# Moving the high and low planes of x into one buffer with longer rows, beside a smaller descriptor scratch

## The chip, the cores and the metric

The kernel runs on one core of a Trainium2 chip. The metric is the device time of one execution in microseconds. Three executions of the kernel before took 2121.49, 2124.33 and 2121.76 us; the median is 2121.76 us.

## What is computed

One step of a decoder layer over 264 tokens: 256 of a prompt and 8 of a sample group. Cut to what matters:

```python
proj = einsum('bld,dk->blk', h, w_in)          # 2048 features -> pool, z, xBC, dt, two gates
pooled = multiscale_pool(u); branch_a = (pooled @ w_pool * pool_scale) @ w_pool_br
y = ssd_chunked(conv(xbc), dt, a, ...) * silu(z), RMS-normed; branch_b = y @ w_ssd_br
out = (sigmoid(g_pool) * branch_a + sigmoid(g_ssd) * branch_b) @ w_out
x = layer_norm(ALPHA * x + out)                # then cross-attention into 256 memory tokens
x = layer_norm(ALPHA * x + attention(x))
x = layer_norm(ALPHA * x + (silu(x @ w_gate) * (x @ w_up)) @ w_down)
```

All of it is float32. The time goes into the products with the large weight matrices; the scans, convolutions and norms run beside them.

## The kernel before, in words

**Layout.** Activations lie feature-major: a feature is a partition, and the 264 tokens lie along the partition. The 2048 features of x are 16 tiles (KT), so x is `[128, 16, ...]`. In what follows a *row* of such a buffer is one tile's stretch of tokens within a partition.

**Products in three parts.** To keep float32 accuracy with the single-pass fp32r format, each operand is split into a high part and the rest, and a product is three matmuls (`mm3`, L392 to L396): x's high row with the weights' high part (L394), x's low row with the same high part (L395), x's high row with the weights' low part (L396). In each the 128x128 block of weights is the stationary operand (an LDWEIGHTS ahead of the matmul) and the row of 264 tokens is the moving one.

**Weights.** 688 units of weights of 128x1024 values (4096 bytes in a partition) stream through a ring of four slots: SyncE loads `raw`, ScalarE rounds it to `whi` (L863), VectorE subtracts to `wlo` (L1390). A unit (L398) is 8 blocks of 128 columns, so 24 matmuls; it waits for `lo_ready` once at its start. In most units 4 rows of x meet two output tiles each (`block_units`, L412), so a row is used by 6 matmuls one after another: high, low, high for one output tile, and again for the other. In the B and C projections a unit takes 8 rows for one output tile (L427).

**The buffers that move.** `xH` and `xL` (L217, L218) are the high and low parts of x: each `[128, 16, 268]` values, rows of 1072 bytes. The last four values of a row are two spare ones and the two gain and bias columns, which 768 of the matmuls take as two more moving columns (266 instead of 264). They are written by ScalarE (`xH`: L872, L1121, L1126, L1133) and VectorE (`xL`: L1405, L1862, L1869, L1923), and read again by VectorE in the residual (L1801, L1803) and the shift (L1824, L1826). Other moving operands of the same three-matmul scheme are `yH`/`yL`, `mixH`/`mixL`, `hH`/`hL`, `oH`/`oL` (rows of 1056 bytes) and `memH`/`memL` (256 tokens, rows of 1024 bytes).

**Addresses in a partition.** The program reserves 8192 bytes at address 0 for the descriptors of DMAs that GpSimd issues (`dynamic_dma_scratch_size`), 128 bytes of constants follow, and then the buffers in the order of `alloc` (L214 on): `raw`, `whi`, `wlo` of 16384 bytes each, `xH` and `xL` of 17152 each, `resid` of 16896, small ones, and at last overlaid buffers that end at 229056 of 229376 bytes. By the order and sizes in the code, `whi` begins at 24704, `wlo` at 41088, `xH` at 57472, `xL` at 74624, `yH` at 115008, `yL` at 148800, `hH` at 125568, `hL` at 172032, `mixH` at 182592, `mixL` at 199488, `memH` at 133760, `memL` at 150144. A block of weights is 512 bytes of a partition, so every block begins at the same place modulo 512.

**Order of the work.** TensorE's program is written out by hand: eight groups of the state-space part (20 units each), the pooling, two branches with their gates (`branch`, L595), the output projection (`project`, L640), the memory attention, the feed-forward pairs (`pair`, L821; 22 pairs of 8 units, all on x), and the down projection on `hH`/`hL`. GpSimd issues the loads and stores of the sample states, the memory caches and some broadcasts (L2186 on); it computes almost nothing.

Of the kernel before, what the change touches and what calls it, by code (L numbers as in the profile page):

```python
# [20 lines left out]
F32R = mybir.dt.float32r  # L21
# [4 lines left out]
P = 128  # L26
# [3 lines left out]
T = SEQ + NSAMP  # L30
KT = D_MODEL // P
# [22 lines left out]
RING = 4  # L54
UNIT = 1024
BLK = 256


VECS = [("conv_w", CT * CONV_W), ("conv_b", CT), ("norm_w", YT), ("d_skip", YT), ("pool_scale", KT),
# [134 lines left out]
def build(nc, a, o):  # L194
    ctx = ExitStack()
    with ctx:
# [3 lines left out]
        def alloc(stack, name, shape, dt=F32):  # L200
            return stack.enter_context(nc.sbuf_tensor("sb_" + name, shape, dt))
# [12 lines left out]
        raw = alloc(ctx, "raw", [P, RING, UNIT])  # L214
        whi = alloc(ctx, "whi", [P, RING, UNIT], F32R)
        wlo = alloc(ctx, "wlo", [P, RING, UNIT], F32R)
        xH = alloc(ctx, "xH", [P, KT, T + 4], F32R)  # L217
        xL = alloc(ctx, "xL", [P, KT, T + 4], F32R)  # L218
        resid = alloc(ctx, "resid", [P, KT, T])
        ident = alloc(ctx, "ident", [P, P])  # L220
        ones_r = alloc(ctx, "ones", [P, P], F32R)
# [164 lines left out]
        def _(pe):  # L386
# [11 lines left out]
            def unit(plan, halfway=None, half_done=None):  # L398

                u = t["unit"]  # L400
                assert u.base % RING == 0 and (u.reg is None or u.per % RING == 0)
                slot = u.k % RING
                pe.wait_ge(lo_ready, u.add() + RING)
                for n, p in enumerate(plan):
                    if halfway and 2 * n == len(plan):
                        halfway()
                    last = mm3(slot, *p)
                    if half_done and 2 * (n + 1) == len(plan):
                        last.then_inc(half_done, 1)
                last.then_inc(used, 1)  # L410

            def block_units(H, L, kts, out, n=T, between=None, before=None, half_done=None):  # L412

                for q in range(0, kts, 4):
# [4 lines left out]
                    if by_tile:  # L419

                        order = [(kk, j) for j in range(2) for kk in range(4)]
                    unit([(kk * BLK + j * P, H[:, q + kk, 0:n], L[:, q + kk, 0:n], out[j][:, 0:n],
                           q + kk == 0, q + kk == kts - 1) for kk, j in order], half_done=by_tile)
# [139 lines left out]
            for e in EVENTS:  # L563
# [22 lines left out]
                else:  # L586

                    pe.wait_ge(s["mix_lo"], e.needs)
                    for b in range(2):
                        unit([(kk * BLK + j * P, mixH[:, e.tile + kk, :], mixL[:, e.tile + kk, :], sets[b][j][:, 0:T],  # L590
                               kk == 0, kk == 3) for kk in range(4) for j in range(2)])
# [36 lines left out]
            def pivot_sum(n):  # L628

                pe.wait_ge(s["res_ready"], 8 * n + 1)  # L630
                pe.matmul(STAT[n][0][:, 0:T], ones[:, :], resid[:, 0, :], start=True, stop=True).then_inc(s["pv_sum"], 1)
# [113 lines left out]
            def values(b, out, between=None):  # L745

                for q in range(4):
                    slot = t["unit"].k % RING
                    pe.wait_ge(lo_ready, t["unit"].add() + RING)
                    for kk in range(4):  # L750
                        for m in range(2):
                            k = 4 * q + kk
                            wH, wL = whi[:, slot, kk * BLK:kk * BLK + BLK], wlo[:, slot, kk * BLK:kk * BLK + BLK]
                            mH, mL = memH[:, k, m * P:m * P + P], memL[:, k, m * P:m * P + P]
                            o_ = out[m][:, 0:BLK]
                            pe.matmul(o_, mH, wH, start=k == 0, stop=False)
# [49 lines left out]
            for b in range(8):  # L806
# [3 lines left out]
                if b == 2:  # L810
                    pivot_sum(1)
                unit([(kk * BLK + j * P, oH[:, kk, :], oL[:, kk, :], out[j][:, 0:T],
                       kk == 0, b == 0 and kk == 3) for kk in range(4) for j in range(2)],
# [30 lines left out]
        def _(act):  # L844
# [313 lines left out]
            def values(b):  # L1158
                finished(4)
                for m in range(2):  # L1160
                    act.activation(Vn[:, m, b * BLK:b * BLK + BLK], SETS[3 * b][m][:, 0:BLK], ACT.Copy)\
                       .then_inc(s["vn_ready"], 1)
# [1301 lines left out]
```

## Time and profile before

| | us |
|---|---|
| three executions | 2121.49, 2124.33, 2121.76 |
| median | 2121.76 |
| profiled execution, first to last instruction (span) | 2119.8 |
| median less that span (what lies around it) | 2.0 |
| granted TensorE clock over the span, share of full speed | 0.998 |

TensorE's matmuls overlap in the profile: one is in flight for some 284 ns, while the next starts some 121 ns after it. So the busy time and the mean duration of a matmul don't say how fast the stream goes. In this document the **gap** is the time from the start of one matmul to the start of the next, and it is read from the start times in the timeline, with the number of matmuls between them from a count over the same window.

### The profile page before, as it was taken

To read this page: it belongs to the slowest core of one execution; us is meant where nothing else is said; L and a number is where in the kernel's file an instruction comes from. 1 tells how busy PE (TensorE), PEld (TensorE's weight loads), DVE (VectorE), ACT (ScalarE), POOL (GpSimd) and SP (SyncE) were. 2 spreads that over 40 slices of the span, in tenths; PEclk is the share of its full clock that TensorE was granted. 3 is DMA by queue.
4 is the path that set the end of the run, shared out by engine and by line. 5 is a ranking of instruction groups with operands and counts; after the bars stand their busy time and mean duration, and the time that the engine had idled before them with its cause. 6 is when DMAs were issued, how large, how long until landed. Compare 5 with 4: busy or idle time off the path is not lost.

```text
span 2119.8 us, 47652 instructions
## 1 busy us (share of the span) xinstructions
PE 2101.2 (99%) x17400; PEld 2084.4 (98%) x17400; DVE 1479.9 (70%) x2393; ACT 1117.5 (53%) x1671; POOL 162.2 (8%) x298
## 2 busy tenths in 40 slices
PE   9999999999999999999999999999999999999997
PEld 8999999999999999999999999999999999999997
DVE  8788877888688988544446876976666666545545
ACT  5566556566545545434444465666656665433333
POOL 1000000000002332000000010001111110000000
PEclk9999999999999999999999999999999999999999
DMA  8655555455557998555556575568888887555553
GB/s 283 191 174 180 190 189 183 160 181 188 187 193 241 314 291 274 178 183 178 178 179 208 181 283 194 165 228 278 279 288 286 271 286 249 175 189 179 180 180 110
DMA packets 125362, 451.78 MB, mean 213 GB/s; under 512 B 16056, under 2 KB 16312, under 8 KB 124232
## 3 DMA queue, kind: packets, MB, share of 16 engines
q1 hardware_dynamic: 101232, 366.41, 50.5%
q0 software_dynamic: 24048, 84.20, 12.8%
q8 instruction: 60, 0.98, 0.2%
q14 instruction: 22, 0.18, 0.0%
HBM read 427.87 MB, written 23.99 MB: 213 GB/s over the span
## 4 chain that ended last, share of the span: by engine, by line
PE 96%; DVE 2%; ACT 1%; DMA 1%; issue 0%; ACTq 0%; POOL 0%; SPq 0%; DVEq 0%
PE G L394 26%; PE G L395 26%; PE G L396 26%; PE M L394 4%; PE M L395 4%; PE M L396 4%; PE M L506 1%; DVE sb_wlo L1390 1%; PE M L518 1%; DMA sb_raw<-in_wstream 0%; DVE sb_resid L1666 0%; ACT sb_whi L863 0%; PE M L509 0%; PE M L489 0%; DMA sb_resid<-in_xT 0%; ACT sb_resid L1362 0%
## 5 line engine op out<-in xcount | busy, mean ns | idle before, releaser
L1390 DVE TENSOR_TENSOR sb_wlo<-sb_raw,sb_whi 128x1024 fp32r<-128x1024 f32 x688 | 834.2, 1223 | 572.4 <-ACT sb_whi L863 570.2
L863 ACT ACTIVATE sb_whi<-sb_raw 128x1024 fp32r<-128x1024 f32 x688 | 721.0, 1057 | 754.8 <-PE G L396 635.6
L394 PE MATMUL G<-sb_xH,sb_whi 128*128 128x264 f32 (+1 forms) x3072 | 874.5, 285 | 1.7 <-DVE sb_wlo L1390 1.1
L396 PE MATMUL G<-sb_xH,sb_wlo 128*128 128x264 f32 (+1 forms) x3072 | 872.5, 284 | 0.0
L395 PE MATMUL G<-sb_xL,sb_whi 128*128 128x264 f32 (+1 forms) x3072 | 872.1, 284 | 0.0
L394 PEld LDWEIGHTS G<-sb_xH,sb_whi 128*128 128x128 f32 x3072 | 578.9, 188 | 4.3 <-issue 2.6
L395 PEld LDWEIGHTS G<-sb_xL,sb_whi 128*128 128x128 f32 x3072 | 578.6, 188 | 0.0
L396 PEld LDWEIGHTS G<-sb_xH,sb_wlo 128*128 128x128 f32 x3072 | 578.5, 188 | 0.0
L395 PE MATMUL G<-sb_hL,sb_whi 128*128 128x264 f32 x704 | 200.2, 284 | 0.0
L396 PE MATMUL G<-sb_hH,sb_wlo 128*128 128x264 f32 x704 | 199.7, 284 | 0.0
L394 PE MATMUL G<-sb_hH,sb_whi 128*128 128x264 f32 x704 | 199.3, 283 | 0.0
L395 PE MATMUL G<-sb_yL,sb_whi 128*128 128x264 f32 x512 | 145.8, 285 | 0.0
L394 PE MATMUL G<-sb_yH,sb_whi 128*128 128x264 f32 x512 | 145.6, 284 | 0.0
L396 PE MATMUL G<-sb_yH,sb_wlo 128*128 128x264 f32 x512 | 145.6, 284 | 0.0
L394 PEld LDWEIGHTS G<-sb_hH,sb_whi 128*128 128x128 f32 x704 | 132.4, 188 | 0.0
L396 PEld LDWEIGHTS G<-sb_hH,sb_wlo 128*128 128x128 f32 x704 | 132.4, 188 | 0.0
L395 PEld LDWEIGHTS G<-sb_hL,sb_whi 128*128 128x128 f32 x704 | 132.1, 188 | 0.0
L394 PE MATMUL M<-sb_xH,sb_whi 128*128 128x264 f32 (+1 forms) x448 | 129.3, 289 | 0.0
L395 PE MATMUL M<-sb_xL,sb_whi 128*128 128x264 f32 (+1 forms) x448 | 127.5, 285 | 0.0
L396 PE MATMUL M<-sb_xH,sb_wlo 128*128 128x264 f32 (+1 forms) x448 | 127.4, 284 | 0.0
L394 PEld LDWEIGHTS G<-sb_yH,sb_whi 128*128 128x128 f32 x512 | 96.6, 189 | 0.0
L395 PEld LDWEIGHTS G<-sb_yL,sb_whi 128*128 128x128 f32 x512 | 96.3, 188 | 0.0
(383 smaller groups left out, 2953.3 us busy)
## 6 DMA issues: line engine op xcount, KB each, us to landing
sb_raw<-in_wstream SPq DMA_DIRECT2D x688, 512.0 KB, 4.0
sb_st<-in_state_ssd POOLq DMA_DIRECT2D x32, 512.0 KB, 6.0
out_new_ssd_s<-sb_st POOLq DMA_DIRECT2D x32, 512.0 KB, 3.8
sb_tmp<-in_state_ssd POOLq DMA_DIRECT2D x34, 256.0 KB, 4.8
sb_cumbc<-scr_cum POOLq DMA_DIRECT2D x8, 1024.0 KB, 4.8
sb_resid<-in_state_ssd POOLq DMA_DIRECT2D x30, 256.0 KB, 4.5
sb_kc<-in_kc POOLq DMA_DIRECT2D x8, 512.0 KB, 9.7
sb_vc<-in_vc POOLq DMA_DIRECT2D x8, 512.0 KB, 5.9
```

The lines of the kernel that those rows point to most:

```text
L394: pe.matmul(out, w, kH, start=start, stop=False)
L395: pe.matmul(out, w, kL, start=False, stop=False)
L396: return pe.matmul(out, wlo[:, slot, col:col + P], kH, start=False, stop=stop)
L506: pe.matmul(outs[h - h0], xdt[:, 0, h * 64:h * 64 + 64], masked_products(h)[:, 0:SEQ], start=True, stop=False)
L518: last = pe.matmul(M[2][:, j * P:j * P + P], xdt[:, b, j * P:j * P + P], Btok[:, b, :], start=b == 0, stop=b == 1)
L863: act.activation(whi[:, slot, :], raw[:, slot, :], ACT.Copy).then_inc(hi_ready, 1)
L1390: dve.tensor_tensor(wlo[:, slot, :], raw[:, slot, :], whi[:, slot, :].bitcast(F32), ALU.subtract)\
```

## The change

`xH` and `xL` become two views of one buffer. Its rows are 576 values (2304 bytes): the high row in the first 288 (1152 bytes), the low row in the other 288. The scratch for GpSimd's descriptors goes from 8192 to 4096 bytes of each partition.

```diff
+HALF_ROW = 288
...
-        xH = alloc(ctx, "xH", [P, KT, T + 4], F32R)
-        xL = alloc(ctx, "xL", [P, KT, T + 4], F32R)
+        xHL = alloc(ctx, "xHL", [P, KT, 2 * HALF_ROW], F32R)
+        xH, xL = xHL[:, :, 0:HALF_ROW], xHL[:, :, HALF_ROW:2 * HALF_ROW]
...
-    nc = bacc.Bacc("TRN2", target_bir_lowering=False, num_devices=1, dynamic_dma_scratch_size=8192)
+    nc = bacc.Bacc("TRN2", target_bir_lowering=False, num_devices=1, dynamic_dma_scratch_size=4096)
```

The two buffers took 34304 bytes of a partition and the new one takes 36864, which is 2560 more. All buffers ahead of it move down by 4096 bytes, all behind it by 1536.

## Rows read from the trace of the kernel before

**Rows 1.** The page: busy time by engine, and the chain that ended last.
```profile
PE 2101.2 (99%) x17400; PEld 2084.4 (98%) x17400; DVE 1479.9 (70%) x2393; ACT 1117.5 (53%) x1671; POOL 162.2 (8%) x298
...
PE 96%; DVE 2%; ACT 1%; DMA 1%; issue 0%; ACTq 0%; POOL 0%; SPq 0%; DVEq 0%
```

**Rows 2.** Groups of TensorE instructions kept apart by shape: count, busy us, mean ns.
```profile
L394 PE MATMUL G<-sb_xH,sb_whi 128*128 128x264 f32 x2944 | 837.6, 285 | 1.2 <-DVE sb_wlo L1390 1.1
L394 PE MATMUL M<-sb_xH,sb_whi 128*128 128x264 f32 x320 | 92.4, 289 | 0.0
L394 PE MATMUL M<-sb_xH,sb_whi 128*128 128x266 f32 x128 | 36.8, 288 | 0.0
L394 PE MATMUL G<-sb_xH,sb_whi 128*128 128x266 f32 x128 | 36.8, 288 | 0.5 <-ACT sb_sgF L1270 0.5
```

**Rows 3.** Busy time and instructions by stretch, all engines.
```profile
1509.60:1835.10 325.50, 325.50 (x2690) 325.50 (x2689) 211.31 (x360) 190.42 (x360) 36.52 (x68) 1.00 0.79 267
1159.50:1212.40 52.90, 52.90 (x434) 52.90 (x433) 41.94 (x53) 28.33 (x36) 0.53 (x1) 1.00 0.62 202
1230.70:1242.20 11.50, 11.50 (x98) 11.50 (x97) 11.40 (x10) 6.31 (x10) 0.00 (x0) 1.00 0.85 328
1369.40:1393.10 23.70, 23.70 (x194) 23.70 (x193) 21.38 (x25) 15.79 (x26) 0.00 (x0) 1.00 0.57 189
```

**Rows 4.** Timeline of TensorE, feed-forward pairs on x: two starts 2688 matmuls apart.
```profile
1509.61 0.28 PE L394 MATMUL G<-sb_xH,sb_whi 128*128 128x264 f32 x1
...
1835.16 0.28 PE L394 MATMUL G<-sb_xH,sb_whi 128*128 128x264 f32 x1
```

**Rows 5.** Timeline, x with 266 columns: two starts 192 matmuls apart.
```profile
1369.44 0.28 PE L394 MATMUL M<-sb_xH,sb_whi 128*128 128x266 f32 x1
...
1393.13 0.28 PE L394 MATMUL G<-sb_xH,sb_whi 128*128 128x266 f32 x1
```

**Rows 6.** Timeline, output projection on mix: two starts 432 matmuls apart.
```profile
1159.51 0.28 PE L394 MATMUL M<-sb_mixH,sb_whi 128*128 128x264 f32 x1
...
1212.43 0.28 PE L394 MATMUL M<-sb_mixH,sb_whi 128*128 128x264 f32 x1
```

**Rows 7.** Timeline, memory projections: 72 matmuls between the first two starts, 96 to the last.
```profile
1230.71 0.28 PE L394 MATMUL M<-sb_memH,sb_whi 128*128 128x256 f32 x1
...
1239.36 0.28 PE L394 MATMUL M<-sb_memH,sb_whi 128*128 128x256 f32 x1
...
1242.23 0.29 PE L394 MATMUL M<-sb_xH,sb_whi 128*128 128x266 f32 x1
```

**Rows 8.** Timeline, row 16 of h: starts 3 and 6 matmuls after the first.
```profile
1858.43 0.28 PE L394 MATMUL G<-sb_hH,sb_whi 128*128 128x264 f32 x1
...
1858.80 0.28 PE L394 MATMUL G<-sb_hH,sb_whi 128*128 128x264 f32 x1
...
1859.17 0.28 PE L394 MATMUL G<-sb_hH,sb_whi 128*128 128x264 f32 x1
```

**Rows 9.** One source line, L396: duration in ns, min/median/max.
```profile
L396 PE MATMUL G<-sb_xH,sb_wlo x3072: 278/284/291, 9.0 to 1846.7; 128*128 128x264 f32 x184, 128*128 128x266 f32 x8
L396 PE MATMUL M<-sb_memH,sb_wlo x32: 283/283/283, 1231.0 to 1242.1; 128*128 128x256 f32 x32
```

**Rows 10.** Longest waits: ScalarE's for TensorE and VectorE's for ScalarE in the weight split.
```profile
ACT sb_whi L863 <- PE G L396: 635.6, 378, 3.9
DVE sb_wlo L1390 <- ACT sb_whi L863: 570.2, 466, 3.6
```

**Rows 11.** GpSimd's DMA issues by group: busy us, mean ns, idle before.
```profile
L2299 POOL DMA_DIRECT2D sb_st<-in_state_ssd x32 | 17.0, 530 | 238.1 <-DMA out_new_ssd_s<-sb_st 121.1 <-DVE sb_xL L1923 106.1 <-issue 11.0
```

## The prediction

> **What bounds the kernel.** I read the page first: TensorE is busy for 99% of the span and carries 96% of the chain that ended last; GpSimd carries 0% of it [rows 1]. Then the groups kept apart by shape, for how much of TensorE's work touches the buffers that move: 3 x (2944 + 320) = 9792 matmuls with 264 moving columns and 3 x (128 + 128) = 768 with 266, so 10560 of 17400, and TensorE waits 1.7 us for anything ahead of the four groups shown [rows 2]. The helpers have room: ScalarE's split waited 635.6 us in total for TensorE to free a slot, VectorE's split 570.2 us for ScalarE [rows 10]. So the time is the number of matmuls times the gap between their starts, at a granted clock of 1.00, which is 2.4 GHz [rows 3], and the change can act through the gap alone.
>
> **The gaps.** Each is two starts and the count between them; the window counts confirm the counts within the two or three that lie over an edge [rows 3].
> - x, 264 columns: (1835.16 - 1509.61) / 2688 = 121.1 ns [rows 4].
> - x, 266 columns: (1393.13 - 1369.44) / 192 = 123.4 ns [rows 5].
> - mix, 264 columns: (1212.43 - 1159.51) / 432 = 122.5 ns [rows 6].
> - mem, 256 columns: (1239.36 - 1230.71) / 72 = 120.1 ns, and to the third start (1242.23 - 1230.71) / 96 = 120.0 ns [rows 7].
>
> What the reader is to see: 264 columns at 2.4 GHz are 110.0 ns and 256 are 106.7 ns, so the gap is 11 to 13 ns over the streaming in every case, and two streams of the same shape, x and mix, differ by 1.4 ns with nothing else to tell them apart than the places of their rows. Other engines are busy to different shares in these stretches, and the mem stretch, where VectorE is busy for 11.40 of 11.50 us, has the shortest gap of all [rows 3]. So the extra comes from TensorE's own reads, and it depends on addresses. I read it as the weight load of the next matmul and the moving row of this one getting in each other's way when they come to the same part of a partition.
>
> **What the change does to the addresses.** Take the beginning of a row less the beginning of a weight block, modulo 256 bytes. For mem it is 0 for every row, high and low (rows of 1024 bytes). For x it steps by 48 from row to row (1072 = 4 x 256 + 48), and is the same for high and low (17152 = 67 x 256). For mix it steps by 32, at places 64 beside those of h. After the change 2304 = 9 x 256, so every high row stands at 0 and, 1152 bytes on, every low row at 128. Whichever buffer precedes moves by 4096 with the weights, so this holds whatever the scratch does. y, mix, h, o and mem move against the weights by 2560 = 10 x 256 and keep their places modulo 256; I cost them at nothing. If the period were 512 or more they would shift too; blocks of weights stand at steps of 512 and of 4096 by slot, and mix repeats its pace over all of them, which speaks for a shorter period.
>
> **The price, bounded.** No row shows a 264-column row at places 0 and 128 over a long stretch. From both sides:
> - Below: matmuls on x last 278 to 291 ns, median 284 [rows 9]. If all took the shortest, the gap would fall by 6 ns: 10560 x 6 = 63 us gained. If all took the longest it would be 7 ns more: 74 us lost. These are the ends for single matmuls, and no long stretch comes near them.
> - Long stretches: between 120.0 (mem) and 122.5 (mix).
> - Nearest by placement: mem, the only stream whose rows all have one place; its matmuls are all alike, 283/283/283 ns, where those on x scatter [rows 9]. A row that always stands the same way to the weights should settle into one repeating pattern. Its 256 columns are 8 fewer, but x with 264 columns has a median of 284 against 283, so the length is not what sets the gap.
> - Nearest by a single row: row 16 of h has its high part at place 0 and its low part at 128, as all rows would have. Its two triples take 0.37 us each, and the six matmuls (1859.17 - 1858.43) / 6 = 123.3 ns, or 122 to 125 as the starts are rounded to 0.01 us [rows 8]. It lasts six matmuls, after rows at other places, so it may show the way in and not the settled pattern.
>
> I take 120.0, because only mem shows what a stream does that keeps one placement.
>
> **The sum.** 9792 x (121.1 - 120.0) = 10.8 us; 768 x (123.4 - 120.0) = 2.6 us; together 13.4 us gained. The writers and readers of the planes on ScalarE and VectorE keep their counts and sizes, only the stride changes: nothing, covered by the waits of [rows 10]; if that cover were gone, TensorE would wait on `lo_ready`. The scratch: GpSimd's issues take 530 ns each and its queue idles 238 us ahead of the state loads alone [rows 11], so issues that wait a little for room delay nothing that TensorE reads; I cost it at nothing. The sum is made against the profiled span of 2119.8, which lies 2.0 us under the median: 2121.76 - 13.4 = 2108.4 us.
>
> **A rule against it.** Rows of x and mix differ in gap at equal shape [rows 4, 6]. The Trainium skill, TensorE: Matmul & The Clock Gate, section "What happens when you issue a matmul", says that TensorE has two independent read ports, so that loading the next weights takes no bandwidth from the running matmul; and its section "Back-to-back issue gap" gives columns / 2.4 + 2.5 ns, by which the gap would be 112.5 ns, whatever the addresses. By it the change moves nothing; the trace contradicts its number by 8.6 ns.
>
> **The rivals.**
> - *Placement averages out* (no change): single matmuls scatter, and a fixed placement may land at the same mean, 121.1 for 264 columns and at most 123.4 for 266: 0 to 2.6 us gained, 2119 to 2122. For it: x and h's mixtures of places have nearly one mean. Against it: mix is 1.4 ns off x.
> - *The row of h is the settled pattern* (slower): place, the alternation of high at 0 and low at 128 in every triple; price, 122.0 (the lower end of the row's reading) to 122.5 ns as in mix: 9792 x 0.9 to 1.4 = 8.8 to 13.7 us lost, less 768 x 1.4 to 0.9 = 1.1 to 0.7 us, so 2129.5 to 2134.8. The point from which it decides is today's mean gap, (9792 x 121.1 + 768 x 123.4) / 10560 = 121.3 ns; it is over 0.2% from 121.3 + 4.2 / 10.56 = 121.7 ns. For it: it is the very placement. Against it: six matmuls.
> - *A deeper lock* (faster): if the fixed placement lets most of the weight load pass between, gaps near the shortest durations, say half of the 6 ns: 32 us, 2090. Nothing long shows it.
> - *The change does nothing on TensorE but starves GpSimd's queue*: the sample states and the broadcast rows come later, VectorE's work with them waits, and with it the weight split. GpSimd's idle time [rows 11] speaks against it; a single stall of each of the 32 pair loads by 0.5 us would be 16 us, hidden unless it exceeds that idle time.
>
> **How the numbers follow.** About 0.2%, 4.2 us, is what a measurement of this kernel can tell from no change. Lock at 120.0: 0.40. Deeper lock: 0.07. Averages out: 0.20. Slower as h's row: 0.26. Slower still (a worse lock than mix, or the queue): 0.07. So faster 0.47, same 0.20, slower 0.33. The likeliest is 2108.4; its own range, for gaps of 119.7 to 120.4, is 2105 to 2113. The range for all takes in h's row and a little of the deeper lock: 2099 to 2136.
>
> **What would show it.** In the changed profile, the starts of the feed-forward pairs on x should lie 120.0 ns apart in a long stretch (right), 121.1 (averages out) or 122.0 and more (h's row). The durations of L394 to L396 on x should collapse to one or three values. Matmuls with 266 columns should have the gap of those with 264. The stretches on y, mix, h and mem should keep their gaps to 0.1 ns; if they don't, the period is not 256 bytes and the model is wrong. GpSimd's waits should be as before.

## The result, and the profile after

The changed kernel takes 2128.05 us (median of 9 runs, 2127.40 to 2128.66), the kernel before in the same comparison 2121.76 us (9 runs): a ratio of 1.003, 95% interval 1.0022 to 1.0039. It is slower by 6.3 us, or 0.3%. I had forecast 2108.4 us, a gain of 13.4; the range to 2136 held the time, the direction was wrong.

The page of the changed kernel, where [rows 1] stood before:

```profile
PE 2106.8 (99%) x17400; PEld 2090.1 (98%) x17400; DVE 1480.4 (70%) x2393; ACT 1118.1 (53%) x1671; POOL 162.4 (8%) x298
...
PE 94%; DVE 3%; DMA 1%; ACT 1%; issue 1%; ACTq 0%; POOL 0%; DVEq 0%; SPq 0%
```

The counts of instructions are those of before, and TensorE is busy for 5.6 us more in a profiled span that grew by 6.4, from 2119.8 to 2126.2 us. So the time went into the gaps between matmuls. The busy time and instructions of the four stretches of [rows 3], in the changed kernel (us of the stretch, then PE, PEld, DVE, ACT, POOL, the granted clock, DMA share, GB/s):

```profile
1514.10:1841.50 327.40, 327.40 (x2691) 327.40 (x2690) 211.41 (x360) 190.74 (x360) 36.54 (x68) 1.00 0.79 265
1163.40:1216.40 53.00, 53.00 (x435) 53.00 (x434) 42.03 (x53) 28.37 (x36) 0.53 (x1) 1.00 0.64 202
1234.60:1246.10 11.50, 11.50 (x98) 11.50 (x97) 11.40 (x10) 6.36 (x10) 0.00 (x0) 1.00 0.83 318
1373.40:1397.10 23.70, 23.70 (x195) 23.70 (x194) 21.37 (x24) 15.81 (x26) 0.00 (x0) 1.00 0.58 185
```

And the timeline of TensorE at the two ends of the same runs of matmuls as before. The two starts of a run are 2688 matmuls apart on x, 192 on x with 266 columns, 432 on mix and 72 on mem:

```profile
1514.14 0.29 PE L395 MATMUL G<-sb_xHL,sb_whi 128*128 128x264 f32 x1
...
1841.48 0.28 PE L395 MATMUL G<-sb_xHL,sb_whi 128*128 128x264 f32 x1
...
1373.41 0.29 PE L395 MATMUL M<-sb_xHL,sb_whi 128*128 128x266 f32 x1
...
1397.09 0.29 PE L395 MATMUL G<-sb_xHL,sb_whi 128*128 128x266 f32 x1
...
1163.43 0.28 PE L395 MATMUL M<-sb_mixH,sb_whi 128*128 128x264 f32 x1
...
1216.35 0.28 PE L395 MATMUL M<-sb_mixH,sb_whi 128*128 128x264 f32 x1
...
1234.63 0.28 PE L395 MATMUL M<-sb_memH,sb_whi 128*128 128x256 f32 x1
...
1243.27 0.28 PE L395 MATMUL M<-sb_memH,sb_whi 128*128 128x256 f32 x1
```

| stream | gap before, ns | gap after, ns |
|---|---|---|
| x, 264 columns, feed-forward | 121.1 [rows 4] | (1841.48 - 1514.14) / 2688 = 121.8 |
| x, 266 columns | 123.4 [rows 5] | (1397.09 - 1373.41) / 192 = 123.3 |
| mix, 264 columns | 122.5 [rows 6] | (1216.35 - 1163.43) / 432 = 122.5 |
| mem, 256 columns | 120.1 [rows 7] | (1243.27 - 1234.63) / 72 = 120.0 |

The work and the granted clock of the 327.40 us stretch are as in [rows 3]; of these four streams only x with 264 columns changed its gap, up by 0.7 ns. The durations on the line that [rows 9] showed:

```profile
L397 PE MATMUL G<-sb_xHL,sb_wlo x3072: 279/285/297, 9.4 to 1853.0; 128*128 128x264 f32 x184, 128*128 128x266 f32 x8
```

They scatter wider than before, not less. The stream does repeat itself, but over 15 matmuls: in the feed-forward stretch the gaps settle into 120, 123, 124, 117, 126, 127, 116, 121, 122, 122, 119, 121, 126, 124, 118 ns and again, give or take one, 1826.7 ns in all, which is 15 x 121.8.

**Where the 6.4 us of span lie.** Taking the starts of all matmuls, stage by stage, after less before: feed-forward on x 2.44 us (152 units of 2922.7 ns against 2906.6), x in the group stage 2.18, x in the pooling stage 0.30, x in the two branches 0.54, x with 266 columns 0.04. These add to 5.5 us on x. The rest is on streams whose buffers kept their places: y in the second branch 0.43, and mix 0.39, almost all of it in the first branch. The output projection on mix, mem and h: 0.00 each. The last 0.07 us lies ahead of the fourth unit, at the start of the kernel. The y stream shows how it comes to 0.43. Its first 96 matmuls, before and then after:

```profile
854.80 0.28 PE L394 MATMUL G<-sb_yH,sb_whi 128*128 128x264 f32 x1
...
866.49 0.28 PE L394 MATMUL G<-sb_yH,sb_whi 128*128 128x264 f32 x1
```

```profile
857.96 0.28 PE L395 MATMUL G<-sb_yH,sb_whi 128*128 128x264 f32 x1
...
869.71 0.28 PE L395 MATMUL G<-sb_yH,sb_whi 128*128 128x264 f32 x1
```

These first 96 take 11.69 us before and 11.75 after, the last 96 of the run 11.76 in both. I read this as y beginning from the pattern that x leaves behind and needing a while to find its own; the run with separate planes, below, shows it.

**GpSimd.** Its waits, where [rows 11] stood before:

```profile
L2300 POOL DMA_DIRECT2D sb_st<-in_state_ssd x32 | 17.0, 530 | 235.7 <-DMA out_new_ssd_s<-sb_st 125.6 <-DVE sb_xHL L1924 106.2 <-issue 3.9
```

An issue takes 530 ns as before and the idle time ahead is 235.7 us against 238.1. Halving the scratch shows nowhere here; the first experiment asks for it alone.

### The profile page after: what moved, and what is told of

It is laid out like the page before. It is cut to its first block, busy times and chain, and to the rows that moved or that the text cites. A ratio compares the mean times of both kernels' runs of the same rounds, so it can differ in the third digit from the quotient of the medians.

```text
span 2126.2 us, 47652 instructions
## 1 busy us (share of the span) xinstructions
PE 2106.8 (99%) x17400; PEld 2090.1 (98%) x17400; DVE 1480.4 (70%) x2393; ACT 1118.1 (53%) x1671; POOL 162.4 (8%) x298
## 4 chain that ended last, share of the span: by engine, by line
PE 94%; DVE 3%; DMA 1%; ACT 1%; issue 1%; ACTq 0%; POOL 0%; DVEq 0%; SPq 0%
PE G L396 26%; PE G L397 26%; PE G L395 26%; PE M L396 4%; PE M L395 4%; PE M L397 4%; DVE sb_wlo L1391 1%; DMA sb_raw<-in_wstream 1%; PE M L507 1%; PE M L519 1%; ACT sb_whi L864 0%; DVE sb_resid L1667 0%; PE M L510 0%; PE M L490 0%; ACT sb_resid L1363 0%
## 5 line engine op out<-in xcount | busy, mean ns | idle before, releaser
L396 PE MATMUL G<-sb_xHL,sb_whi 128*128 128x264 f32 (+1 forms) x3072 | 877.0, 285 | 0.0
L397 PE MATMUL G<-sb_xHL,sb_wlo 128*128 128x264 f32 (+1 forms) x3072 | 875.8, 285 | 0.0
L395 PE MATMUL G<-sb_xHL,sb_whi 128*128 128x264 f32 (+1 forms) x3072 | 871.3, 284 | 2.6 <-DVE sb_wlo L1391 2.1
L395 PEld LDWEIGHTS G<-sb_xHL,sb_whi 128*128 128x128 f32 x3072 | 582.8, 190 | 5.0 <-issue 3.1
L397 PEld LDWEIGHTS G<-sb_xHL,sb_wlo 128*128 128x128 f32 x3072 | 580.2, 189 | 0.0
L396 PEld LDWEIGHTS G<-sb_xHL,sb_whi 128*128 128x128 f32 x3072 | 577.4, 188 | 0.0
L396 PE MATMUL G<-sb_hL,sb_whi 128*128 128x264 f32 x704 | 200.2, 284 | 0.0
L396 PE MATMUL G<-sb_yL,sb_whi 128*128 128x264 f32 x512 | 146.0, 285 | 0.0
L396 PEld LDWEIGHTS G<-sb_hL,sb_whi 128*128 128x128 f32 x704 | 132.1, 188 | 0.0
L395 PE MATMUL M<-sb_xHL,sb_whi 128*128 128x264 f32 (+1 forms) x448 | 128.8, 288 | 0.0
L397 PE MATMUL M<-sb_xHL,sb_wlo 128*128 128x264 f32 (+1 forms) x448 | 128.0, 286 | 0.0
L396 PE MATMUL M<-sb_xHL,sb_whi 128*128 128x264 f32 (+1 forms) x448 | 128.0, 286 | 0.0
L397 PEld LDWEIGHTS G<-sb_yH,sb_wlo 128*128 128x128 f32 x512 | 96.4, 188 | 0.0
```

Of the source, the lines that this page charges most:

```text
L395: pe.matmul(out, w, kH, start=start, stop=False)
L396: pe.matmul(out, w, kL, start=False, stop=False)
L397: return pe.matmul(out, wlo[:, slot, col:col + P], kH, start=False, stop=stop)
```

## The experiments

The theory after the result: the settled gap belongs to the pair of places (of the high row, of the low row), in bytes modulo 256, and not to whether there is one place. mem has the pair (0, 0), the changed x the pair (0, 128). The rivals: the scratch costs something; the side-by-side layout itself costs; the longer rows cost; the length of 264 columns makes the difference to mem.

### The scratch alone

```diff
 # the kernel before
-    nc = bacc.Bacc("TRN2", target_bir_lowering=False, num_devices=1, dynamic_dma_scratch_size=8192)
+    nc = bacc.Bacc("TRN2", target_bir_lowering=False, num_devices=1, dynamic_dma_scratch_size=4096)
```

> The kernel before with the scratch at 4096 bytes and the two planes as they were. Placement theory (gaps of TensorE depend on where the moving row stands against the weight block modulo 256 bytes): every buffer moves by 4096 together, nothing changes, 2121.8 us within 0.1%. Scratch theory (GpSimd's queue lacks room for descriptors): the whole loss of the change is here, about 2128 us, with longer waits on GpSimd's issues.

Measured: 2121.18 against 2121.79 us, ratio 0.9998 (0.9989 to 1.0007). The feed-forward stretch, two starts 2688 matmuls apart:

```profile
1509.24 0.28 PE L394 MATMUL G<-sb_xH,sb_whi 128*128 128x264 f32 x1
...
1834.79 0.28 PE L394 MATMUL G<-sb_xH,sb_whi 128*128 128x264 f32 x1
```

That is 121.1 ns as before, and no stage after the start differs from the kernel before by more than 0.2 us. So the scratch costs nothing that can be measured here, and the loss is in the rows.

### Side by side, with rows of 2144 bytes

```diff
 # the changed kernel, scratch of 8192
-HALF_ROW = 288
+HALF_ROW = T + 4
```

> Side by side with the scratch left at 8192: rows of 2144 bytes, the low row 1072 bytes behind the high one. High rows step by 96 modulo 256, low rows stand 48 beyond them. Placement theory: places are mixed again as in the kernel before, so the gap is near 121.1 to 121.4 ns and the time 2120 to 2125 us, and the place modulo 256 of y, mix, h and mem against the weights is as before (the new buffer is as long as the two old ones). Theory that side by side itself costs: 2128 us as in the changed kernel.

Measured: 2123.59 us, ratio 1.0008 (0.9999 to 1.0018). The timeline of TensorE in the feed-forward stretch, two starts 2688 matmuls apart:

```profile
1510.78 0.29 PE L395 MATMUL G<-sb_xHL,sb_whi 128*128 128x264 f32 x1
...
1837.07 0.29 PE L395 MATMUL G<-sb_xHL,sb_whi 128*128 128x264 f32 x1
```

That is 121.39 ns, between before (121.1) and the change (121.8). The time and the gap are in the range expected. By the medians, two planes in one buffer without the padding lose less than a third of what the change loses, 1.8 us of 6.3, and the interval still holds no loss at all. That the gap comes out near before's, with places that go round, is what the placement theory says; what mean to expect from places that go round is another matter, taken up with the map.

### The padding, with separate planes

```diff
 # the changed kernel
-        xHL = alloc(ctx, "xHL", [P, KT, 2 * HALF_ROW], F32R)
-        xH, xL = xHL[:, :, 0:HALF_ROW], xHL[:, :, HALF_ROW:2 * HALF_ROW]
+        xH = alloc(ctx, "xH", [P, KT, HALF_ROW], F32R)
+        xL = alloc(ctx, "xL", [P, KT, HALF_ROW], F32R)
```

Rows of 1152 bytes (4 x 256 + 128) take the pairs (0, 0) and (128, 128) in turn.

> Two separate planes with rows of 1152 bytes and the scratch at 4096: high and low rows stand together at 0 for even rows and at 128 for odd rows. Placement theory: a different time from the changed kernel's 2128, since high and low have one place instead of two; by the rows of mem it would be faster (gap 120.0, 2108 us), by mere averaging 2122. Theory that the longer rows or side by side as such cost: as the changed kernel (longer rows) or as before (side by side).

Measured: 2127.39 us, ratio 1.0027 (1.0016 to 1.0037). In the feed-forward stretch, 2688 matmuls apart:

```profile
1513.33 0.29 PE L395 MATMUL G<-sb_xH,sb_whi 128*128 128x264 f32 x1
...
1840.37 0.29 PE L395 MATMUL G<-sb_xH,sb_whi 128*128 128x264 f32 x1
```

121.67 ns: nearly the whole loss is there without any side-by-side layout, and the time is neither of the two that I had expected under the placement theory, 2108 and 2122 us. So neither the one buffer nor the short way from high to low row is needed for it. What is left is the places or the longer rows; the placements further down, with rows of 2304 bytes, decide for the places.

This run also settles the y stream. y and mix stand at the very addresses that they have in the changed kernel, since the two planes are as long as its one buffer. The first 96 matmuls of y:

```profile
857.35 0.29 PE L395 MATMUL G<-sb_yH,sb_whi 128*128 128x264 f32 x1
...
869.05 0.28 PE L395 MATMUL G<-sb_yH,sb_whi 128*128 128x264 f32 x1
```

They take 11.70 us where the changed kernel needs 11.75, and over the span y loses 0.06 us to before instead of 0.43, mix 0.04 instead of 0.39. So those losses came from what x had run before, and not from the new addresses of y and mix.

### A map of all pairs of places

A kernel of its own: four slots of weights are loaded and split once, and TensorE runs 48 matmuls in the kernel's order at each of the 16 x 16 pairs of places in steps of 16 bytes. Its core, with `high` and `low` in those steps:

```diff
+def stretch(high, low, n, triples):
+    for i in range(triples):
+        k, j = i // 2 % 4, i % 2
+        col = (k * 2 + j) * P
+        h, l = 4 * high, 384 + 4 * low
+        out = G[:, j, 0:n]
+        pe.matmul(out, whi[:, k, col:col + P], x[:, k, h:h + n], start=True, stop=False)
+        pe.matmul(out, whi[:, k, col:col + P], x[:, k, l:l + n], start=False, stop=False)
+        pe.matmul(out, wlo[:, k, col:col + P], x[:, k, h:h + n], start=False, stop=True)
```

> A kernel that leaves all of the decoder step out and only measures gaps: three-matmul products without a wait, 48 matmuls for each pair of places (high row at 0 to 240, low row at 0 to 240, in steps of 16 bytes modulo 256 against the weight blocks), 264 columns, then 256 to 272 columns at four pairs. Placement theory: the gap settles into a repeating pattern for each pair, 121.8 ns for (0, 128) as in the changed kernel, and differs over pairs by some ns; for (0, 0) with 256 columns 120.0. Theory that other engines or the order of the kernel's work make the gap: one gap for all pairs, near 112 ns.

Measured: 1651.02 us, one execution. Timeline of TensorE, from 18 matmuls into a stretch, when its pattern has settled, to the first of the next, 30 matmuls later, for the pairs (0, 0), (0, 128), (128, 128) and (240, 144):

```profile
35.82 0.28 PE L246 MATMUL G<-sb_x,sb_whi 128*128 128x264 f32 x1
39.42 0.28 PE L246 MATMUL G<-sb_x,sb_whi 128*128 128x264 f32 x1
...
82.25 0.28 PE L246 MATMUL G<-sb_x,sb_whi 128*128 128x264 f32 x1
85.91 0.28 PE L246 MATMUL G<-sb_x,sb_whi 128*128 128x264 f32 x1
...
828.35 0.29 PE L246 MATMUL G<-sb_x,sb_whi 128*128 128x264 f32 x1
832.05 0.29 PE L246 MATMUL G<-sb_x,sb_whi 128*128 128x264 f32 x1
...
1488.83 0.28 PE L246 MATMUL G<-sb_x,sb_whi 128*128 128x264 f32 x1
1492.37 0.28 PE L246 MATMUL G<-sb_x,sb_whi 128*128 128x264 f32 x1
```

(0, 0): 3.60 / 30 = 120.0 ns at 264 columns, the same as mem with 256. (0, 128): 3.66 / 30, with the starts taken finer 121.8, the gap of the changed kernel. (128, 128): 123.3. (240, 144): 117.8, the lowest of all. The map's mean is 121.5, and 56 of the 256 pairs are at 120.0 or under it. So a row that keeps one pair has the gap of its pair, and the pair (0, 128), at 121.77, is 0.2 ns worse than the mean of the map, 121.53.

The length is not out of it, though. The same kernel goes on with other lengths, and the pair (0, 128) with 256 columns, again 30 matmuls apart, has

```profile
1535.17 0.28 PE L246 MATMUL G<-sb_x,sb_whi 128*128 128x256 f32 x1
...
1538.67 0.28 PE L246 MATMUL G<-sb_x,sb_whi 128*128 128x256 f32 x1
```

116.7 ns, where (0, 0) with 256 columns has the 120.0 of mem. So at the length of mem the order of the two pairs is the reverse: the price belongs to pair and length together. And (0, 0) at 264 columns, right behind a stretch of 260 columns, settled at 121.3 ns: even this pair has a second pattern.

For rows whose places go round the map gives no price. Its mean over the 16 pairs of the old rows (high and low at the same place) is 121.0, where the kernel before has 121.1; but for the eight pairs of mix, also high and low at the same place, it is 121.2, where the output projection takes 122.5, and for the rows of 2144 bytes 121.9, where 121.4 was measured. Separate planes agree in the mean, 121.65 by (0, 0) and (128, 128) against 121.67, but not row by row: by the starts of the 152 units, six matmuls at (0, 0) take 122.3 ns each there and six at (128, 128) 121.0, the reverse of the map. That agreement may be chance.

### Three placements taken from the map

All three start from the changed kernel and move only where the rows begin; the third also sets 224 bytes ahead of the buffer and 32 behind it.

```diff
 # low row at 1200 bytes: places (0, 176), where the map has 120.0
+        xH, xL = xHL[:, :, 0:T + 4], xHL[:, :, 300:300 + T + 4]
 # rows at 48 and 1168 bytes: places (48, 144), where the map has 120.0
+        xH, xL = xHL[:, :, 12:12 + T + 4], xHL[:, :, 292:292 + T + 4]
 # places (240, 144), where the map has 117.8
+        alloc(ctx, "lead", [P, 56])
         xHL = alloc(ctx, "xHL", [P, KT, 2 * HALF_ROW], F32R)
+        xH, xL = xHL[:, :, 4:4 + T + 4], xHL[:, :, 300:300 + T + 4]
+        alloc(ctx, "trail", [P, 8])
```

> The changed kernel with one thing moved: the low row begins 1200 bytes behind the high one instead of 1152, so high rows stand at 0 and low rows at 176 modulo 256. Same buffer, same row length, same scratch. Placement theory, by the map (48 matmuls at this pair took 120.6 ns each, the last 30 of them 120.0): the gap in the feed-forward stretch is 120.0, against 121.8 in the changed kernel; 9792 x 1.8 ns = 18 us less than 2128 us, about 2110 us. Rival (row length or side by side costs, or the map doesn't carry over to a kernel with waits and other engines at work): 2128 us.

> The changed kernel with the high row 48 bytes and the low row 1168 bytes into each row of 2304, so high rows at 48 and low rows at 144 modulo 256, with no bytes before or after the buffer. Placement theory, by the map (120.2 ns over 48 matmuls, 120.0 over the last 30): gap 120.0, about 2110 us. Theory that only beginnings at a multiple of 64 bytes are good: slower than the kernel before, since 48 is none.

> The changed kernel with 224 bytes ahead of the buffer and 32 behind it, the high row 16 bytes and the low row 1200 bytes into each row of 2304: high rows at 240, low rows at 144 modulo 256, everything else where it was modulo 256. Placement theory, by the map (118.2 ns over 48 matmuls, 117.8 over the last 30, the least of 256 pairs): a gap near 117.8 in the long stretches on x, 9792 x 4.0 ns = 39 us less than the changed kernel, about 2089 us. If that pattern is only reached from some starts (the map entered each pair once), the gap is 120 to 122 and the time 2110 to 2128 us.

| places | median, us | ratio to before (95%) | feed-forward gap, ns |
|---|---|---|---|
| (0, 176) | 2111.37 | 0.995 (0.9937 to 0.9964) | 120.0 |
| (48, 144) | 2111.45 | 0.9952 (0.9939 to 0.9966) | 120.0 |
| (240, 144) | 2097.21 | 0.9886 (0.9871 to 0.9901) | 117.8 |

Timeline of the feed-forward stretch with places (0, 176), starts 2688 matmuls apart:

```profile
1502.89 0.28 PE L395 MATMUL G<-sb_xHL,sb_whi 128*128 128x264 f32 x1
...
1825.45 0.28 PE L395 MATMUL G<-sb_xHL,sb_whi 128*128 128x264 f32 x1
```

The same with places (240, 144):

```profile
1493.67 0.28 PE L397 MATMUL G<-sb_xHL,sb_whi 128*128 128x264 f32 x1
...
1810.26 0.28 PE L397 MATMUL G<-sb_xHL,sb_whi 128*128 128x264 f32 x1
```

Its stretch (columns as above), and its page:

```profile
1493.60:1810.20 316.60, 316.60 (x2690) 316.60 (x2690) 211.36 (x360) 190.56 (x360) 36.56 (x69) 1.00 0.81 275
```

```profile
PE 2076.0 (99%) x17400; PEld 2059.0 (98%) x17400; DVE 1479.7 (71%) x2393; ACT 1117.6 (53%) x1671; POOL 161.9 (8%) x298
```

What the reader is to see: moving where the rows begin, with not one instruction more or less, takes the same 2688 matmuls from 327.3 to 322.6 or 316.6 us, at the same granted clock of 1.00, and the page's TensorE busy time falls from 2106.8 to 2076.0 us. The first two come out at the forecast of 2110 within 1.5 us, with rows as long as in the changed kernel, so the longer rows aren't the cause. (48, 144) begins no row at a multiple of 64 bytes and is as fast as (0, 176), so aligned rows are not the point.

The third is the fastest kernel of this study: 24.5 us under the kernel before and 31 under the change. It missed its own forecast of 2089 by 8 us. The gap of 117.8 holds in the feed-forward stretch, but not in the group stage, where small products stand between the stretches on x. One such stretch, two starts 119 matmuls apart:

```profile
189.03 0.37 PE L397 MATMUL G<-sb_xHL,sb_whi 128*128 128x264 f32 x1
...
203.66 0.28 PE L399 MATMUL G<-sb_xHL,sb_wlo 128*128 128x264 f32 x1
```

That is 122.9 ns, and the three others of a round take 119.3, 120.9 and 118.9, the same in every round from the second on. On the 6144 matmuls on x with 264 columns outside the feed-forward stretch, 4.0 ns each would have been 24.6 us under the change; 14.4 came. The price of a pair is therefore sure only in a long unbroken stretch.

### The map again, in the opposite order

The kernel of the map with the pairs in reverse, 266 columns for 176 of them, and then the pairs (0, 0), (0, 128) and (240, 144) with 128, 96 and 64 columns of weights.

> The map of gaps again, with the pairs in the reverse order, so that each is entered from another pattern; then 266 columns for low rows 48 to 208 bytes beyond the high ones modulo 256; then 264 columns with weight blocks of 128, 96 and 64 columns at three pairs. It leaves all of the decoder step out. If the gap follows from the places alone, all 256 pairs repeat to 0.3 ns; if the start counts too, some pairs fall into another pattern (120.0 against 121.4 or 122.2). If the weight load is what gets in the way of the moving row, the gap shrinks with the columns of the weight block, toward 264 / 2.4 = 110 ns; if it is a fixed cost of a matmul, it stays.

Measured: 2364.62 us, one execution. 194 of the 256 pairs come within 0.3 ns of the first map, (0, 0), (0, 128) and (0, 176) among them. The others settle elsewhere, reached from another side. The pair (240, 144), 30 matmuls again:

```profile
65.25 0.28 PE L246 MATMUL G<-sb_x,sb_whi 128*128 128x264 f32 x1
...
68.92 0.28 PE L246 MATMUL G<-sb_x,sb_whi 128*128 128x264 f32 x1
```

122.2 ns, where the first map had 117.8: the same addresses, the same work, another entry. This fits what cost the fastest kernel its 8 us, whose broken stretches lie between these two values. With 266 columns the pairs lie between 120.0 and 128.9 ns; (0, 128) has 123.1 and (0, 176) 122.2.

The narrow weights, by groups of weight loads (count, busy us, mean ns) and by the timeline; the starts are those of the (0, 0) stretch with 96 columns, of the next stretch, and of the same two with 64:

```profile
L246 PEld LDWEIGHTS G<-sb_x,sb_whi 128*128 128x128 f32 x6272 | 1184.1, 189 | 20.3 <-DVE sb_wlo L232 20.3
L246 PEld LDWEIGHTS G<-sb_x,sb_whi 128*96 128x96 f32 x48 | 7.8, 162 | 0.0
L246 PEld LDWEIGHTS G<-sb_x,sb_whi 128*64 128x64 f32 x48 | 6.4, 134 | 0.0
```

```profile
2322.53 0.28 PE L246 MATMUL G<-sb_x,sb_whi 128*96 128x264 f32 x1
2328.29 0.28 PE L246 MATMUL G<-sb_x,sb_whi 128*96 128x264 f32 x1
...
2339.92 0.28 PE L246 MATMUL G<-sb_x,sb_whi 128*64 128x264 f32 x1
2345.68 0.28 PE L246 MATMUL G<-sb_x,sb_whi 128*64 128x264 f32 x1
```

A weight load of 64 columns is 55 ns shorter than one of 128, and the 48 matmuls take 5.76 us with 96 and with 64 columns, 120.0 ns each, as with 128; (0, 128) has 121.8, 121.5 and 121.8 ns with 128, 96 and 64 columns. So for these two pairs the extra time doesn't scale with the length of the weight load, as it would if load and moving row were in each other's way for as long as both run. That form of my reading in the prediction isn't borne out. The third pair decides nothing: (240, 144) has 122.1, 120.6 and 117.8 ns, which looks like a fall with the width, but the first and the last are the two gaps that it has with 128 columns too.

### Which addresses count

96 matmuls a stretch, the last 48 measured. It moves the blocks of weights against fixed rows, and changes accumulators, banks and weight slots.

```diff
+wh, wl = flat(whi[:, :, :]), flat(wlo[:, :, :])
-col = (k * 2 + j) * P
+col = 4 * weights + (k * 2 + i % 2) * P + (0 if one else k % 3 * 1024)
-out = G[:, j, 0:n]
+out = G[:, i % banks, at:at + n]
```

> Which addresses count. Gaps again with no decoder step around them, 96 matmuls to a stretch, at four pairs of places (0, 0), (0, 128), (0, 176), (240, 144): the weight blocks moved by 16 to 192 bytes with the rows left alone; the product's columns in the accumulators moved by 8 to 32; one accumulator bank and not two in turn; all weights from one ring slot; every matmul a product of its own and not one of three added up. Then lengths from 128 to 288 columns at (0, 0) and (240, 144). My reading of the kernel before (weight load against moving row, so only their difference counts): moving the weights changes the gap as moving both rows would, and the accumulators change nothing. Rival (the place of the moving rows alone counts, and their length): moving the weights changes nothing. For the lengths: if the gap is streaming plus a fixed cost it grows by 0.417 ns a column; if it is quantised, it goes in steps of 6.7 ns or of a third of that per matmul.

Measured: 1043.62 us, one execution, with these gaps (ns):

| weights moved by, bytes | 0 | 16 | 32 | 64 | 96 | 128 | 176 | 192 |
|---|---|---|---|---|---|---|---|---|
| (0, 0) | 120.0 | 122.2 | 120.0 | 120.1 | 121.5 | 123.3 | 120.0 | 120.0 |
| (0, 128) | 121.7 | 121.6 | 122.3 | 121.5 | 123.0 | 124.4 | 121.2 | 121.6 |
| (240, 144) | 117.9 | 122.2 | 121.2 | 121.5 | 120.9 | 122.2 | 120.7 | 121.6 |

Two of these cells in the timeline, starts 48 matmuls apart: (0, 0) with the weights in place, and moved by 128 bytes.

```profile
28.63 0.28 PE L248 MATMUL G<-sb_x,sb_whi 128*128 128x264 f32 x1
34.39 0.28 PE L248 MATMUL G<-sb_x,sb_whi 128*128 128x264 f32 x1
...
86.79 0.29 PE L248 MATMUL G<-sb_x,sb_whi 128*128 128x264 f32 x1
92.71 0.28 PE L248 MATMUL G<-sb_x,sb_whi 128*128 128x264 f32 x1
```

Moving the weights by 128 bytes gives 5.92 / 48 = 123.3 ns, just what the map has where both rows are at 128 instead. With (0, 176) as a fourth pair there are 20 shifts by a multiple of 32 bytes, and each of the 20 lands within 0.35 ns of one of the two maps at the pair that the shift leads to; held against pairs of the maps at random, 5 of the 20 would. Of the 8 shifts by 16 or 176 bytes, 2 do. So the place relative to the weights, as the prediction defined it, is the right variable in steps of 32 bytes, and in finer steps the weights' own address counts too. The accumulator moved by 8, 16 or 32 columns, one bank for two, one weight slot for three, each matmul a product of its own: 120.0 ns in all at (0, 0), 121.6 to 121.9 at (0, 128), 117.8 at (240, 144). The accumulators and the slot of the weights have no part in it.

The same kernel with other lengths, at (0, 0) and (240, 144): 111.7 ns from 128 to 232 columns in both; 112.0 and 112.7 at 240, 120.0 and 117.8 at 264, 131.7 and 135.6 at 288. From 128 to 232 columns these two pairs don't differ.

## Why the prediction was wrong

**What bounds the kernel: right.** TensorE's gap was what moved; count and clock stayed. Of the 6.4 us of span, 5.5 are gaps on x by the sum above.

**The address as the cause: right, and shown.** Moving rows alone took the kernel from 2128.05 to 2111.37 and 2097.21 us. The period of 256 bytes fits too, but not for the reason that the prediction gave. It says that y, mix, h and mem would shift if the period were 512; they moved by 2560 bytes, which is 5 x 512 as well, so their steady gaps (output projection on mix, mem and h, to 0.1 ns) can't tell 256 from 512. What speaks for 256 is that the rows of the changed kernel, 2304 bytes apart, alternate between two places modulo 512, the rows of the map, 3072 apart, don't, and both have 121.8 ns. By the test of the prediction itself, y and mix in the branches would even have refuted the model, with the 0.43 and 0.39 us that they lost; the run with separate planes shows that their addresses had no part in it.

**The step that failed** is in "The price, bounded": "I take 120.0, because only mem shows what a stream does that keeps one placement." It took having one placement for the cause of mem's low gap. What counts is which pair: mem's rows are at (0, 0), the changed ones at (0, 128). The map prices them at 120.0 and 121.8 ns at 264 columns. Setting the length aside failed too: with mem's 256 columns (0, 128) takes 116.7 ns, so mem's 120.0 wasn't even a low gap for its length. The term 9792 x (121.1 - 120.0) = 10.8 us gained came out as a loss: by the feed-forward gaps to the hundredth 9792 x (121.78 - 121.11) = 6.6 us, by the sum over the stages 5.5. The second term, 768 x (123.4 - 120.0) = 2.6 us gained, was nothing: 266 columns at (0, 128) take 123.3 ns. The prediction named the row of h as the very placement and set it aside because it lasts six matmuls. It pointed to the right side (by the starts taken finer it is at 122.0 ns, not 123.3), but not as a price: six matmuls within rows at other places don't show a pair's settled gap, as the six at (0, 0) on separate planes show with 122.3 ns where the settled gap is 120.0. No row of before had a settled stream at (0, 128), so nothing there could tell 120.0 from 121.8. The range held the time because it took in this rival, not because the step that gave the forecast was sound.

**"A row that always stands the same way to the weights should settle into one repeating pattern": right**, but a repeating pattern isn't a short one. "The durations should collapse to one or three values" failed: 279 to 297 ns, a repeat of 15. So did "Matmuls with 266 columns should have the gap of those with 264": 123.3 against 121.8 ns. With places (0, 176), where the gap is 120.0, the repeat is three matmuls.

**The rivals.** *The row of h is the settled pattern* came nearest, on the right side, with a price a little too high: 122.0 to 122.5 ns gave 2129.5 to 2134.8, the settled gap is 121.8 and the time 2128.05. *Placement averages out* isn't borne out: the fixed pair has 121.8 and not 121.1. As for the mixed rows, x before is near the mean of its 16 pairs (121.0 in the first map, 121.4 in the second), but mix, at 122.5, is not near that of its eight (121.2 and 121.7). *A deeper lock* exists: 117.8 ns at (240, 144), with a time of 2097.21, but not at this change's pair. The starved queue is ruled out by the run with the scratch alone.

**Costed at nothing.** The scratch: right. y and mix in the branches: wrong by 0.43 and 0.39 us, since they start from the pattern that x leaves; I hadn't priced what one stream passes on to the next.

**The rule against it.** The Trainium skill, TensorE: Matmul & The Clock Gate, section "Back-to-back issue gap", gives an isolated gap of columns / 2.4 + 2.5 ns. No stream of these products agrees with it: with 264 columns they take 117.8 to 126.7 ns where it gives 112.5, and with 128 columns 111.7 where it gives 55.8. The same section warns that with a weight load per matmul the formula counts too little at short lengths, which fits in direction; its own figure of about 81 ns at 128 columns isn't met either.

**Open.** Why a pair has the gap that it has, and what sets the gap of rows whose places go round. The runs show that the place of the rows against the weights, their length and what ran before matter; none shows the mechanism.

## What to carry to other kernels

Where TensorE streams without a wait and reloads weights for each matmul, the places of the moving rows against the weight blocks modulo 256 bytes can be worth 1%, as here with 264 columns, and moving them costs nothing. But alignment isn't the aim, and the pair has to be measured, because round placements came out both ways here, from 120.0 ns at (0, 0) to 123.3 at (128, 128). When a price is carried over from another stream, check that it has the same pair and the same length, and not only the same regularity. If no stream has them, the price is unknown: a few matmuls at the right pair amid others don't give it either. A kernel that runs the one configuration by itself does, and then it has to be confirmed in the kernel itself: a gap from the map held to 0.1 ns in the unbroken stretch, and not in stages with interruptions.

## What the runs showed of the hardware that I had not expected

- The gap has a floor of 111.7 ns for 128 columns of weights, flat from 128 to 232 moving columns at the two pairs measured. From 240 to 288 columns it rises for (0, 0) from 112.0 to 131.7 ns, by about what 48 columns take at 2.4 GHz (20.0 ns), but unevenly: 113.3 at 248, 116.7 at 252, 120.0 at 256, 118.6 at 260, 120.0 at 264.
- Many settled gaps lie on steps. 122.2, 120.0 and 121.1 ns, 1.11 apart, are the commonest values of the map, and the patterns read closely close on a multiple of 6.67 ns: 360.0 ns for three matmuls at (0, 176), 353.3 for three at (240, 144), 1826.7 for 15 in the changed kernel.
- The same pair can hold two patterns. (240, 144) ran at 117.8 and at 122.2 ns, (96, 96) at 121.7 and 126.7, (0, 0) at 120.0 and 121.3, by what ran before it, and a later stream at fixed addresses inherits some of this (y: 11.70 against 11.75 us for its first 96 matmuls, at the same addresses after other places of x).
